# Gated DeltaNet inverse: D product of the first level in 32-column tiles, and a chunk's two token products as one matmul

## The chip, the cores and the metric

The kernel runs on one core of one Trainium2 chip. The metric is the device time of an execution in microseconds (us).

## What is computed

The reference is one inference step of a two-layer hybrid trunk of width 2048: a gated DeltaNet layer, then a Mamba-2 SSD layer, for a prompt of 256 tokens and for 8 sequences of 4 new tokens each. The change lies in the DeltaNet layer's work on the prompt. For each of 16 key heads (two value heads each), in chunks of tokens, it is

```python
a_mat = einsum("bnhid,bnhjd->bnhij", k_beta, k) * decay * strict
t_mat = triangular_solve(eye + a_mat, eye, lower=True, unit_diagonal=True)
u = t_mat @ (v * beta);  w = t_mat @ (k_beta * exp(g))
qk = einsum("bnhid,bnhjd->bnhij", q, k) * decay
```

and then a recurrence over the chunks. The products of keys with keys and of queries with keys, and the inverse of a unit triangular matrix, are what the two edits touch.

## The kernel before

Each engine has its own program, written out by hand, with semaphores between them. The DeltaNet stage is a loop over heads m: 15 turns of a loop and a last head written out behind it. All projections go through the same steps: a half tile of weights (128 x 1024) arrives by DMA, ScalarE takes its upper part (L826), GpSimd (POOL) the rest (L336), and TensorE (PE) does three matmuls of 288 columns for each of 16 slices (L381 to L383, in `project`).

PE's loop counts 48 steps e in a head. In each it does `project` for two slices (six matmuls), and behind it, by the number of the step, a piece of the head's own work in `gdn_mix`. So everything on PE has one order. The pieces that matter here:

- e = 0: token products. `gKN` holds the normalised queries and keys (first index 0 and 1) with 128 rows and the tokens as columns; NC = 2 chunks of CH = 128 tokens. Per chunk there is a transpose of the keys to psA (L446), a product of keys with keys to psC (L447) and one of keys with queries to psC from column 256 on (L448); then a small product for the new tokens (L449), which raises `g_tok`. The vector engine (DVE) multiplies both into its arrays at L1582 and L1586.
- e = 5: transposes of `gDE` to psB (L455), which ScalarE copies (L1017).
- e = 7 to 18: the inverse, in six levels lv, over four matrices u (two chunks, two value heads). At e = 7 + 2 lv PE does the P product to psC (`inv_p`). DVE masks it (`mask_p`, L1609). At e = 8 + 2 lv PE does the D product to psA and then the E product to psE (`inv_q`), and DVE subtracts them (`less_q`, L1621 and L1628). Between these DVE puts independent taps of a convolution (L1600). `do.link` makes DVE's next instruction wait for the end of the one that is linked.
- e = 8 also has, ahead of the D product of the first level, two small transposes of 32 rows (L460).

All three products of the levels 0 to 4 go through one helper, whose matmul is L408:

```python
def blocks(bank, u, lhsT, rhs, lv, n=64):
    for r in range(0, P, n):
        mm = pe.matmul(bank[r:r + n, u * 32:(u + 1) * 32], lhsT[:, r:r + n], rhs[:, in_block(r, lv), :],
                       start=True, stop=True)
```

The output rows r to r + n are a column tile of the array. The P product has n = 32, the D and E products n = 64; each matmul has 32 moving columns. In the profile "128*64" is contraction rows by weight columns of one matmul. A fp32 matmul appears there as two passes, each with its own weight load (PEld); a transpose appears as one.

Of the kernel before, what the change touches and what calls it, by code (L numbers as in the profile page):

```python
# [30 lines left out]
CH = 128  # L31
NC = SEQ // CH
# [62 lines left out]
def bc(ap, axis, n):  # L95
    a = ap.unsqueeze(axis)
    shape = list(a.shape)
    shape[axis] = n
    return a.to_broadcast(shape)


def half(ap, lv, odd):

    v = ap.rearrange("p j (i k s) -> p j i k s", k=2, s=2 << lv)
    return v[:, :, :, odd, :]
# [7 lines left out]
def in_block(r, lv):  # L113

    n = 32 // (2 << lv)
    return slice(r // 64 * n, r // 64 * n + n)
# [25 lines left out]
def build(nc, weights, x_in, p_in, prm_in, cst_in, gpack, spack, gstate, sstate,  # L142
          y_out, gconv_out, sconv_out, gst_p, gst_s, sst_p, sst_s,
          g_rows, s_rows, h_spill, G_DVE, G_ACT, S_DVE, S_ACT):
    with ExitStack() as ctx:
# [3 lines left out]
        def sem(name):  # L149
# [17 lines left out]
        psA, psB, psC, psD, psE, psF = (  # L167
            ctx.enter_context(nc.psum_tensor(f"ps{c}", [P, 512], F32)) for c in "ABCDEF")
# [25 lines left out]
        gKN = ga["KN"].rearrange("p (i t) -> p i t", i=2)  # L194
# [21 lines left out]
        gP = [gPP, gPZ[:, 0], gPZ[:, 1], gPZ[:, 2], gPW, gPW]  # L216

        gDE = ga["DE"].rearrange("p (k u t) -> p k u t", k=2, u=4)
# [73 lines left out]
        def S(name):  # L292
            if name not in sems:
                sems[name] = sem(name)
            return sems[name]
# [74 lines left out]
        def _(pe):  # L370
# [34 lines left out]
# [5 lines that stand above are left out]
                return mm  # L410
# [28 lines left out]
            def gdn_mix(m, e, more):  # L439

                if e == 0:
                    pe.wait_ge(S("g_kn"), m + 1)
                    pe.wait_ge(S("g_y"), m + 1)
                    for c in range(NC):
                        k_c, q_c = (gKN[:, n, c * CH:(c + 1) * CH] for n in (1, 0))
                        pe.transpose(psA[:, c * P:(c + 1) * P], k_c, ident)  # L446
                        pe.matmul(psC[:, c * CH:(c + 1) * CH], k_c, k_c, start=True, stop=True)  # L447
                        pe.matmul(psC[:, 256 + c * CH:256 + (c + 1) * CH], k_c, q_c, start=True, stop=True)  # L448
                    pe.matmul(psE[0:NS, 0:2 * NS], gKN[:, 1, SEQ:T], gKN[:, 0:2, SEQ:T], start=True, stop=True) \  # L449
                        .then_inc(S("g_tok"), 1)  # L450
                if e == 5:
                    pe.wait_ge(S("g_e1"), m + 1)
                    for c in range(NC):
                        for j in range(2):
                            mm = pe.transpose(psB[:, (2 * c + j) * P:(2 * c + j + 1) * P], gDE[:, 1, 2 * c + j, :],  # L455
                                              ident)
                    mm.then_inc(S("g_dt"), 1)
                if e == 8:
                    for j in range(2):
                        mm = pe.transpose(psD[0:NS, 384 + NS * j:384 + NS * (j + 1)], gATS[:, j, :], ident[0:NS, 0:NS])  # L460
# [17 lines left out]
                def inv_q(lv):  # L478


                    pe.wait_ge(S("g_pm"), m * 6 + lv + 1)
                    if lv < 5:
                        for u in range(4):
                            mm = blocks(psA, u, gDE[:, 1, u, :], half(gP[lv], lv, 0)[:, u], lv)
                        mm.then_inc(S("g_qd"), 1)
                    for u in range(4):
                        E = half(gDE[:, 1], lv, 1)[:, u]
                        if lv < 5:
                            mm = blocks(psE, u, gP[lv][:, u, :], E, lv)
                        else:  # L490
                            mm = pe.matmul(psE[0:64, u * 64:(u + 1) * 64], gP[lv][:, u, 0:64], E, start=True, stop=True)
                    mm.then_inc(S("g_qe"), 1)

                for lv in range(6):
                    if e == 7 + 2 * lv:
                        inv_p(lv)
                    if e == 8 + 2 * lv:
                        inv_q(lv)
                if e == 10:
                    for j in range(2):  # L500
                        mm = pe.matmul(psD[0:NS, 256 + NS * j:256 + NS * (j + 1)], gATS[:, j, :], gAS[:, j, :],
                                       start=True, stop=True)
                    mm.then_inc(S("g_sample_pe"), 1)
                if e == 15:
                    for j in range(2):
                        mm = pe.matmul(psD[NS * j:NS * j + NS, 320:320 + NS], gBS[:, j, :], gNS[:, j, :],
                                       start=True, stop=True)
                    mm.then_inc(S("g_sample_pe"), 1)
                if e == 18:
# [5 lines left out]
                    for b in range(DEC_B):  # L515
                        for j in range(2):
                            mm = pe.matmul(psD[64 * j:64 * j + 64, 0:P], gMKQ[:, b, :], gS[:, b, j, :],
                                           start=(b == 0), stop=(b == DEC_B - 1))
                    mm.then_inc(S("g_sample_pe"), 1)
                if e == 17:  # L520
# [3 lines left out]
                    for c in range(NC):  # L524
                        for j in range(2):
                            mm = pe.transpose(psB[:, (2 * c + j) * P:(2 * c + j + 1) * P],
                                              gCR[:, 2 + j, c * CH:(c + 1) * CH], ident)
# [12 lines left out]
                if e == 23:  # L540
                    pe.wait_ge(S("g_es"), m + 1)
                    pe.wait_ge(S("g_rss"), m + 1)
                    for j in range(2):
                        rows = slice(NS * j, NS * j + NS)
                        mm = pe.matmul((psA, psB)[j][:, 0:P], gES[rows], gVBS[rows], start=True, stop=True)
# [10 lines left out]
                if e == 27:  # L556
                    pe.wait_ge(S("g_rhs"), m + 1)
                    new_values(1)
                    for j in range(2):
                        mm = pe.matmul(psD[NS * (2 + j):NS * (3 + j), 256:256 + P], gQKS[:, j, :],  # L560
                                       gVNS[:, j * P:(j + 1) * P], start=True, stop=True)
# [3 lines left out]
                if e == 29:  # L565
# [3 lines left out]
                    for j in range(2):  # L569
                        o = psF[:, (2 + j) * P:(3 + j) * P]  # L570
                        pe.matmul(o, gQD[:, j, :], gS1[:, j, :], start=True, stop=False)
                        mm = pe.matmul(o, gQK[:, 2 + j, :], gVN[:, 2 + j, :], start=False, stop=True)
                    mm.then_inc(S("g_o"), 1)
                if e == 30:
# [4 lines left out]
                    for r in range(2):  # L579
                        for g in range(4):  # L580
                            rows = slice(NS * g, NS * g + NS)
                            mm = pe.matmul((psA, psB, psC, psD)[g][:, r * 256:(r + 1) * 256], gKM[rows, r, :],
                                           gVNDS[rows, :], start=True, stop=True)
                    mm.then_inc(S("g_sp"), 1)
                if e == 41:
                    pe.wait_ge(S("g_on"), m + 1)
                    for j in range(2):
                        for c in range(NC):
# [3 lines left out]
                              start=True, stop=True).then_inc(S("g_ont"), 1)  # L592
# [15 lines left out]
            for n in range(4):  # L608
                for c in range(NC):
                    src = HRG[0:GV, (7, 6, 4, 5)[n], c * CH:(c + 1) * CH]  # L610
                    at = (n * NC + c) * GV
                    mm = pe.transpose(psD[:, at:at + GV], src, ident[0:GV, 0:GV])
            for n in range(5):
                src = HRG[0:GV, (7, 6, 4, 8, 5)[n], SEQ:T]
                for g in range(4):
                    mm = pe.matmul(psD[NS * g:NS * g + NS, 256 + n * GV:256 + (n + 1) * GV], src, ident[0:GV, 0:GV],
                                   start=True, stop=True)
            mm.then_inc(S("g_ccol"), 1)
            with pe.Fori(0, GH - 1) as m:
                for e in range(48):  # L620
                    if e % 8 == 0:
                        bank_wait_act(m, 6, T_GLOOP + e // 8, T_GPRO, TA_G)
                    gdn_ready(m, e)
                    project(m, 6, T_GLOOP + e // 8, e % 8)
                    gdn_mix(m, e, True)

            for e in range(48):
                k = e // 8
                if e % 8 == 0:
                    if k < 4:  # L630
                        bank_wait_act(0, 0, T_GEND + k, T_GPRO, TA_G)
                    else:
                        pe.wait_ge(took_dve, TD_O1 + (k - 3))
                if e < 16 or e >= 20:
                    gdn_ready(GH - 1, e if e < 16 else e - 4)
                project(0, 0, T_GEND + k, e % 8, fresh=X0["oa1"] if k == 2 else None)
                if e < 16:
                    gdn_mix(GH - 1, e, False)
                elif e >= 20:
                    gdn_mix(GH - 1, e - 4, False)  # L640
# [142 lines left out]
            for k in range(2, 7):  # L783
# [4 lines left out]
                if k == 4:  # L788
                    pe.wait_ge(S("s_hrows"), 1)
                    for n in range(3):  # L790
                        for c in range(NC):
                            src = HRG[0:SH, (4, 6, 5)[n], c * CH:(c + 1) * CH]
                            at = (n * NC + c) * SH
                            mm = pe.transpose(psA[:, at:at + SH], src, ident[0:SH, 0:SH])
# [631 lines left out]
        def _(dve):  # L1426
# [136 lines left out]
            def u4(ap):  # L1563
                return ap.rearrange("p (c j) t -> p c j t", c=NC)
# [12 lines left out]
            def gdn_body(m, full):  # L1577

                dve.wait_ge(S("g_tok"), m + 1)
                kk = bc(psC[:, 0:256].rearrange("p (c t) -> p c t", c=NC), 2, 2)  # L1580
                qk = bc(psC[:, 256:512].rearrange("p (c t) -> p c t", c=NC), 2, 2)
                do.link(dve.tensor_tensor(u4(gAT[:, :, :]), u4(gAT[:, :, :]), kk, ALU.mult))  # L1582
                do.link(dve.tensor_tensor(gPW, gAT[:, :, :], bc(cst[:, K_M1, :], 1, 4), ALU.mult))
                dve.tensor_tensor(gDE[:, 1], bc(ident, 1, 4), gPW, ALU.subtract) \
# [194 lines left out]
            with dve.Fori(0, GH - 1) as m:  # L1779
                do.enter(m, G_DVE)  # L1780
                gdn_body(m, True)
                dve.wait_ge(took_act, m * 6 + 12)
            do.leave(GH - 1)
            gdn_body(GH - 1, False)


# [432 lines left out]
```

## Time and profile before

| | |
|---|---|
| median of 3 runs | 2421.05 us (2419.09 to 2421.67) |
| profiled execution | 2421.49 us |
| its span, first to last instruction | 2419.7 us |
| mean granted TensorE clock | 0.989 |
| PE, weight loads | 2327.6 and 2183.3 us busy |
| DVE, ACT, POOL | 1615.2, 1263.9 and 1795.1 us busy |

The page is one profiled execution. Busy shares are over the whole span; the DeltaNet loop is the part from about 83 to 1035 us. In a timeline row several instructions of a kind that follow each other are merged, with their count; the time in the row then goes from the first start to the last end.

### The profile page before, as it was taken

What the parts mean: (1) busy time and instruction counts of PE and PEld (TensorE: products, weight loads), DVE (VectorE), ACT (ScalarE), POOL (GpSimd) and SP (SyncE); (2) the same over time, 40 slices, a digit from 0 to 9 for tenths busy, and PEclk for the clock granted to TensorE, in tenths of its full rate; (3) what the DMA queues carried; (4) which work ended last, traced back from release to release, by engine and by line L of the source; (5) the groups of instructions that cost most, each with busy time, mean ns of one, the idle gap of its engine ahead of it and who ended that gap; (6) DMA issues with size and microseconds to landing.
All of it is one profiled execution on the core that took longest, in us unless ns stands there. A gap on an engine that the chain in (4) does not pass through costs nothing.

```text
span 2419.7 us, 59342 instructions
## 1 busy us (share of the span) xinstructions
PE 2327.6 (96%) x21792; PEld 2183.3 (90%) x21792; DVE 1615.2 (67%) x3171; ACT 1263.9 (52%) x2204; POOL 1795.1 (74%) x2284
## 2 busy tenths in 40 slices
PE   5899999999999999999999979999999999999997
PEld 5799999999999999989999978999999999899997
DVE  7667666666666676661217576988899889703375
ACT  4555555555555555543336456555555555433452
POOL 4566666565555556558889967988898889798896
PEclk9999999999999999999999989999999999999998
DMA  5444444444444444436454446766676657454443
GB/s 197 156 150 156 157 152 154 148 150 144 147 154 150 146 142 148 147 120 220 153 169 148 160 150 205 233 207 192 205 244 212 203 185 240 173 194 156 155 155 117
DMA packets 126775, 410.88 MB, mean 170 GB/s; under 512 B 21344, under 2 KB 37984, under 8 KB 122112
## 3 DMA queue, kind: packets, MB, share of 16 engines
q1 hardware_dynamic: 80784, 294.49, 36.6%
q10 hardware_dynamic: 45936, 115.64, 14.2%
q8 instruction: 37, 0.61, 0.1%
q14 instruction: 18, 0.15, 0.0%
HBM read 363.47 MB, written 46.61 MB: 169 GB/s over the span
## 4 chain that ended last, share of the span: by engine, by line
POOL 37%; PE 32%; issue 23%; DVE 6%; ACT 1%; POOLq 0%; DMA 0%; DVEq 0%; ACTq 0%
POOL wl L336 36%; PE psj L381 9%; PE psj L383 9%; PE psj L382 9%; POOL h L344 1%; DVE h L2003 1%; PE psE L403 1%; PE psE L747 1%; PE psA L721 1%; PE psA L773 1%; DVE arena L1876 0%; DVE arena L1526 0%; DVE arena L2034 0%; DVE xl L1810 0%; DVE xl L1451 0%
## 5 line engine op out<-in xcount | busy, mean ns | idle before, releaser
L336 POOL TENSOR_TENSOR wl<-ring,wh 128x256 fp32r<-128x256 f32 x2232 | 1761.9, 824 | 602.5 <-ACT wh L826 602.2
L381 PE MATMUL psj<-xh,wh 128*128 128x288 f32 x4400 | 1356.9, 308 | 32.6 <-DVE xl L1451 16.5
L382 PE MATMUL psj<-xl,wh 128*128 128x288 f32 x4400 | 1304.1, 296 | 0.0
L383 PE MATMUL psj<-xh,wl 128*128 128x288 f32 x4400 | 1299.3, 295 | 0.0
L381 PEld LDWEIGHTS psj<-xh,wh 128*128 128x128 f32 x4400 | 830.6, 189 | 84.5 <-issue 43.9
L826 ACT ACTIVATE wh<-ring 128x1024 fp32r<-128x1024 f32 x558 | 586.6, 1059 | 600.4 <-PE psj L383 529.4
L382 PEld LDWEIGHTS psj<-xl,wh 128*128 128x128 f32 x4400 | 833.4, 189 | 1.9
L383 PEld LDWEIGHTS psj<-xh,wl 128*128 128x128 f32 x4400 | 834.1, 190 | 0.0
L907 ACT ACTIVATE arena<-psj 128x256 f32<-128x256 f32 x112 | 42.8, 382 | 191.9 <-PE psj L383 186.2
L1802 DVE TENSOR_TENSOR h<-h,psj 128x288 f32 x32 | 14.5, 454 | 155.6 <-PE psj L383 155.6
L1876 DVE SCALAR_TENSOR_TENSOR arena<-arena 128x256 f32<-128x256 f32 x144 | 111.2, 799 | 3.4
L1600 DVE SCALAR_TENSOR_TENSOR arena<-arena 128x256 f32<-128x256 f32 (+1 forms) x192 | 103.5, 559 | 4.1
L1792 DVE COPY Y<-psj 128x288 f32 x22 | 10.1, 458 | 131.5 <-PE psj L383 131.5
L1526 DVE SCALAR_TENSOR_TENSOR arena<-arena 128x256 f32<-128x256 f32 x192 | 80.7, 481 | 1.6
L1497 DVE TENSOR_TENSOR arena<-arena 128x288 f32<-128x288 f32 x45 | 29.4, 653 | 72.2 <-ACT arena L1184 66.5
L1609 DVE TENSOR_TENSOR arena<-psC,cst 64x128 f32<-64x128 f32 (+1 forms) x176 | 53.0, 301 | 21.4 <-PE psC L408 12.0
L2003 DVE TENSOR_TENSOR h<-h,arena 128x512 f32<-128x512 f32 x64 | 63.6, 994 | 0.0
L408 PEld LDWEIGHTS psA<-arena 128*64 128x64 f32 x1280 | 43.8, 137 | 18.6 <-DVE arena L1609 15.0
L408 PE MATMUL psA<-arena 128*64 128x32 f32 x1280 | 52.7, 225 | 4.9 <-DVE arena L1609 4.0
L1621 DVE TENSOR_TENSOR arena<-arena,psA 64x128 f32<-64x128 f32 x160 | 45.7, 285 | 15.0 <-PE psA L408 6.7
L408 PE MATMUL psE<-arena 128*64 128x32 f32 x1280 | 51.0, 223 | 0.0
L408 PEld LDWEIGHTS psE<-arena 128*64 128x64 f32 x1280 | 44.2, 138 | 0.0
(344 smaller groups left out, 2943.5 us busy)
## 6 DMA issues: line engine op xcount, KB each, us to landing
ring<-weights_d SPq DMA_DIRECT2D x558, 512.0 KB, 3.3
h<-gstate_d ACTq DMA_DIRECT2D x16, 1024.0 KB, 7.0
gst_s_d<-h ACTq DMA_DIRECT2D x16, 1024.0 KB, 3.9
h<-sstate_d ACTq DMA_DIRECT2D x32, 512.0 KB, 5.6
sst_s_d<-h ACTq DMA_DIRECT2D x32, 512.0 KB, 5.1
arena<-g_rows_d ACTq DMA_DIRECT2D x16, 864.0 KB, 5.8
arena<-s_rows_d ACTq DMA_DIRECT2D x8, 1152.0 KB, 8.4
h_spill_d<-h ACTq DMA_DIRECT2D x2, 2304.0 KB, 8.2
```

What stands on the lines that cost most here:

```text
L336: ins = pool.tensor_tensor(wl[:, s, n:n + 2], ring[:, s, n:n + 2], wh[:, s, n:n + 2].bitcast(F32), ALU.subtract)
L381: pe.matmul(out, w_h, xh[:, kt, :], start=(kt == 0), stop=False)
L382: pe.matmul(out, w_h, xl[:, kt, :], start=False, stop=False)
L383: mm = pe.matmul(out, w_l, xh[:, kt, :], start=False, stop=(kt == KT - 1))
L408: mm = pe.matmul(bank[r:r + n, u * 32:(u + 1) * 32], lhsT[:, r:r + n], rhs[:, in_block(r, lv), :], start=True, stop=True)
L826: act.activation(wh[:, hc % 4], ring[:, hc % 4], ACT.Copy).then_inc(wh_ready, 1)
L1526: ins = dve.scalar_tensor_tensor(out, src, tap(i, j), out, ALU.mult, ALU.add)
L1600: return dve.scalar_tensor_tensor(out, gU[:, 2 + i, at:at + b - a], gpc_tap[1][:, i, j:j + 1], out, ALU.mult, ALU.add)
L1609: ins = dve.tensor_tensor(half(gP[lv][rows], lv, 0)[:, :, blk, :], packed(psC[rows, 0:(P if lv < 5 else 2 * P)], lv), half(bc(cst[rows, K_ ...
L1621: ins = dve.tensor_tensor(D, D, packed(psA[rows, 0:P], lv), ALU.subtract)
L1876: ins = dve.scalar_tensor_tensor(out, src, w, out, ALU.mult, ALU.add)
L2003: do.link(dve.tensor_tensor(sS[:, b], sS[:, b], bc(sEGb[:, :, b], 2, HD), ALU.mult))
```

## The change

Two edits. The D product of the first level (lv = 0) is made with n = 32, in four column tiles for each matrix, in place of two. And for each chunk one matmul takes the keys as weights and moves queries and keys (256 columns) past them, in place of two matmuls with 128 columns each; its output lies in psC as query part and key part, chunk by chunk, and DVE's two reads of it have the new strides.

```diff
--- before.py
+++ after.py
@@ -442,10 +442,10 @@
                     pe.wait_ge(S("g_kn"), m + 1)
                     pe.wait_ge(S("g_y"), m + 1)
                     for c in range(NC):
-                        k_c, q_c = (gKN[:, n, c * CH:(c + 1) * CH] for n in (1, 0))
+                        k_c = gKN[:, 1, c * CH:(c + 1) * CH]
                         pe.transpose(psA[:, c * P:(c + 1) * P], k_c, ident)
-                        pe.matmul(psC[:, c * CH:(c + 1) * CH], k_c, k_c, start=True, stop=True)
-                        pe.matmul(psC[:, 256 + c * CH:256 + (c + 1) * CH], k_c, q_c, start=True, stop=True)
+                        pe.matmul(psC[:, c * 256:(c + 1) * 256], k_c, gKN[:, 0:2, c * CH:(c + 1) * CH],
+                                  start=True, stop=True)
                     pe.matmul(psE[0:NS, 0:2 * NS], gKN[:, 1, SEQ:T], gKN[:, 0:2, SEQ:T], start=True, stop=True) \
                         .then_inc(S("g_tok"), 1)
                 if e == 5:
@@ -481,7 +481,7 @@
                     pe.wait_ge(S("g_pm"), m * 6 + lv + 1)
                     if lv < 5:
                         for u in range(4):
-                            mm = blocks(psA, u, gDE[:, 1, u, :], half(gP[lv], lv, 0)[:, u], lv)
+                            mm = blocks(psA, u, gDE[:, 1, u, :], half(gP[lv], lv, 0)[:, u], lv, 32 if lv < 1 else 64)
                         mm.then_inc(S("g_qd"), 1)
                     for u in range(4):
                         E = half(gDE[:, 1], lv, 1)[:, u]
@@ -1577,8 +1577,7 @@
             def gdn_body(m, full):
 
                 dve.wait_ge(S("g_tok"), m + 1)
-                kk = bc(psC[:, 0:256].rearrange("p (c t) -> p c t", c=NC), 2, 2)
-                qk = bc(psC[:, 256:512].rearrange("p (c t) -> p c t", c=NC), 2, 2)
+                qk, kk = (bc(psC[:, :].rearrange("p (c n t) -> p c n t", c=NC, n=2)[:, :, n, :], 2, 2) for n in range(2))
                 do.link(dve.tensor_tensor(u4(gAT[:, :, :]), u4(gAT[:, :, :]), kk, ALU.mult))
                 do.link(dve.tensor_tensor(gPW, gAT[:, :, :], bc(cst[:, K_M1, :], 1, 4), ALU.mult))
                 dve.tensor_tensor(gDE[:, 1], bc(ident, 1, 4), gPW, ALU.subtract) \
```

## Rows read from the trace of the kernel before

**Rows 1.** The page: engines, and the chain that ended last by engine

```profile
PE 2327.6 (96%) x21792; PEld 2183.3 (90%) x21792; DVE 1615.2 (67%) x3171; ACT 1263.9 (52%) x2204; POOL 1795.1 (74%) x2284
...
POOL 37%; PE 32%; issue 23%; DVE 6%; ACT 1%; POOLq 0%; DMA 0%; DVEq 0%; ACTq 0%
```

**Rows 2.** Windows by stage: us, busy time and instructions by engine, clock, DMA, GB/s

```profile
83.00:1035.00 952.00, 942.03 (x11286) 862.61 (x11285) 660.41 (x1733) 540.39 (x1045) 581.78 (x768) 1.00 0.45 151
```

**Rows 3.** Waits of 83 to 1035 us: us in total, times, longest

```profile
PEld psA L408 <- DVE arena L1609: 14.0, 44, 0.5
...
DVE arena L1621 <- PE psA L408: 5.7, 19, 0.9
```

**Rows 4.** Timeline, token products, head 7: start, us, engine, line, passes [idle, releaser]

```profile
467.64 0.29 PE L383 MATMUL psj<-xh,wl 128*128 128x288 f32 x1
467.77 0.27 PE L446 MATMUL psA<-cst,arena 128*128 128x128 f32 x1
467.88 0.39 PE L447 MATMUL psC<-arena 128*128 128x128 f32 x2
468.11 0.39 PE L448 MATMUL psC<-arena 128*128 128x128 f32 x2
468.33 0.27 PE L446 MATMUL psA<-cst,arena 128*128 128x128 f32 x1
...
468.66 0.39 PE L448 MATMUL psC<-arena 128*128 128x128 f32 x2
468.98 0.30 PE L449 MATMUL psE<-arena 128*32 128x64 f32 x2
```

**Rows 5.** Timeline of PE, same head: a two-pass product with 256 columns

```profile
511.95 0.59 PE L567 MATMUL psE<-arena 128*128 128x256 f32 x2
512.38 0.38 PE L571 MATMUL psF<-arena 128*128 128x128 f32 x2
512.60 0.39 PE L572 MATMUL psF<-arena 128*128 128x128 f32 x2
```

**Rows 6.** Timeline of the same head, first level of the inverse

```profile
475.41 0.46 PE L408 MATMUL psC<-arena 128*32 128x32 f32 x32
...
475.95 0.60 DVE L1609 TENSOR_TENSOR arena<-psC,cst 64x128 f32<-64x128 f32 x2 [0.66 <-PE psC L408]
...
476.57 1.03 DVE L1600 SCALAR_TENSOR_TENSOR arena<-arena 128x256 f32<-128x256 f32 x1
...
476.79 0.23 PE L460 MATMUL psD<-cst,arena 32*32 32x32 f32 x2
...
476.95 0.66 PE L408 MATMUL psA<-arena 128*64 128x32 f32 x16
...
477.44 0.64 PE L408 MATMUL psE<-arena 128*64 128x32 f32 x16
477.74 0.58 DVE L1621 TENSOR_TENSOR arena<-arena,psA 64x128 f32<-64x128 f32 x2
...
478.35 0.59 DVE L1628 TENSOR_TENSOR arena<-arena,psE 64x128 f32<-64x128 f32 x2
...
478.97 0.65 DVE L1600 SCALAR_TENSOR_TENSOR arena<-arena 128x32 f32<-128x32 f32 x1
...
479.74 0.59 DVE L1609 TENSOR_TENSOR arena<-psC,cst 64x128 f32<-64x128 f32 x2
```

**Rows 7.** Timeline of weight loads for psA, L408: heads 1, 8 and 10

```profile
99.69 0.55 PEld L408 LDWEIGHTS psA<-arena 128*64 128x64 f32 x16
...
110.20 0.55 PEld L408 LDWEIGHTS psA<-arena 128*64 128x64 f32 x16 [0.16 <-DVE arena L1609]
...
539.90 0.55 PEld L408 LDWEIGHTS psA<-arena 128*64 128x64 f32 x16
...
550.90 0.55 PEld L408 LDWEIGHTS psA<-arena 128*64 128x64 f32 x16 [0.48 <-DVE arena L1609]
...
665.79 0.55 PEld L408 LDWEIGHTS psA<-arena 128*64 128x64 f32 x16
```

## The prediction, made before the changed kernel was built or run

> **What bounds the kernel now.** I read the page first: TensorE (the engine PE) is busy for 96% of the span [rows 1]. Both edited places lie in the head loop of the DeltaNet stage, so the second view was the windows by stage. From 83 to 1035 us PE is busy for 942.0 of 952 us at full granted clock, and POOL for 582 [rows 2]. The page's chain gives POOL the largest share [rows 1]; in this stage that is not the bound, because POOL has 370 us of the 952 left over. The loop goes at the pace of PE's own queue.
>
> The third view was the list of waits. Two entries matter in the edited steps. The weight loads of the bank psA at L408 waited for the vector engine's mask at L1609 44 times, 14.0 us in all, and the vector engine waited at L1621 for the same bank 19 times, 5.7 us [rows 3]. So inside the inverse the two engines take turns in being late, and it has to be worked out which of them an edit there speeds up.
>
> **Part 1, token products.** Now a chunk has one transpose (a single pass) and two products of two passes each, five passes of 128 moving columns. The first chunk runs from 467.77 to 468.33 us, thus 0.56/5 = 0.112 us a pass [rows 4]. The change removes the two passes of L448 and makes those of L447 256 columns wide. What a 256-column pass costs is not seen at this line, but at L567: its two passes run from 511.95 to 512.38, thus 0.215 us each, and the pair after it, of 128 columns, takes 0.22 us, or 0.11 each [rows 5]. So a fp32 pass is paid by its moving columns, and what is saved is only what each pass has on top. Per head: 8 x 0.112 = 0.90 us become 4 x 0.215 = 0.86 us, **0.04 us less**. With 0.11 in place of 0.112 it is 0.02. I take 0.04; the bounds are 0 and 0.06. The weight load that disappears was hidden under the pass before it and is costed at nothing. Were it not hidden, the whole pass could be saved (first rival).
>
> Nothing takes these 0.04 us back. The products stand in PE's queue, the products of the first level come 7.5 us later, and there the vector engine waits for PE (0.66 us of idle time at 475.95) [rows 6], so its chain moves forward by the same 0.04 us. L1582 and L1586 read as many elements of psC as before, at another stride: nothing, with bounds of 0.02 us either way, and there is that idle time of 0.66 us to cover it.
>
> **Part 2, D product of the first level.** Now it is 16 passes with 64 columns of weights, which hold PE from 476.95 to 477.44, 0.49 us. The changed one has the shape of the P product, 32 passes with 32 columns of weights. That one stands at 475.41 with 0.46 us for all, of which a single pass is 0.20: the last starts about 0.26 us after the first [rows 6]. Behind it the tile shape changes from 32 to 64 columns for the E product in psE. The nearest row for that change is the one from L460 to L408, 0.16 us with its two passes [rows 6]; the low end is L449, which comes 0.32 us behind the pair before it, where a pair takes 0.22, so 0.10 us [rows 4]. Now no such change stands between the two products; the one between L460 and the D product exists in both kernels. So the phase becomes 0.26 + 0.13 = 0.39 us (0.13 between the two ends), **0.10 us less on PE**.
>
> The Trainium skill has a rule against this edit: in "TensorEngine Tiling (Array Packing)", section Tiling Modes, a change of tiling mode (not of tile alone) drains TensorE. The trace agrees in kind, with the 0.16 us above. If draining meant that the last pass ends (0.20 us) before the next load begins, the phase would be about 0.26 + 0.36 = 0.62 us, and the E product would come 0.13 us later than now; by the next paragraph only the first head would feel it, and the sum would be 0.2 us higher.
>
> **How much of it stays on the path.** The vector engine's chain from the first mask on is: mask 475.95 to 476.55, tap 476.57 to 477.60, D subtraction from 477.74 [rows 6]. The tap has nothing to do with the D product, and the next linked tap (478.97 to 479.62) shows 0.12 us from its end to the start behind it (479.74), where PE had long been done. So the D subtraction can start at 477.72: 0.02 us earlier, with bounds of 0 and 0.14. From there to the mask of the fourth level this engine goes from one instruction to the next, and PE waits for it. The D products of the first and the fourth level stand 11.00 us apart (539.90 and 550.90), in the first head, where the vector engine keeps up, 10.51 us (99.69 and 110.20) [rows 7]. So PE loses 0.49 us a head there; the 0.48 us of idle time in the last row has some 0.16 in it that the change of tile shape takes anyway, as the first head's row shows. So whatever PE gains in the first level is added to that loss: of the 0.10 us about 0.08 is given back at the second to fourth level, and **0.02 us a head** stay. Only the first head keeps all of it. The same slack covers a longer drain: the E product ends at 478.08 and its subtraction starts at 478.35, when the D subtraction has ended.
>
> **Sum.** 16 x (0.04 + 0.02) = 0.96, and 0.08 for the first head: about 1.0 us less. The stages after the loop start that much earlier and are otherwise as before. The profiled execution took 2421.49 us (span 2419.7), which is 0.4 above the median of the runs shown, so the sum holds for the median as well: 2421.05 - 1.0 = 2420.0 us. These three runs lie 2.6 us apart, so the effect is smaller than their scatter.
>
> **Rivals.**
> First, a merged pass is cheaper than I think: if the 0.112 us of a 128-column pass were set by its weight load, a 256-column pass would cost the same and L448's four passes a head would go entirely: 4 x 0.112 x 16 = 7.2 us, with part 2 7.6: 2413.4 us, faster. For it speaks that the projections move 288 columns in 0.13 us [rows 4], which is more than twice as fast by column. Against it speaks L567, fp32 operands as here, at 0.215 us a pass. Chance 4%. The Trainium skill gives this rival its rule: "TensorE: Matmul & The Clock Gate", Back-to-back issue gap and LDWEIGHTS, has N/2.4 + 2.5 ns for N columns and P/1.2 ns for P columns of weights, so 109 ns for 256 columns and 107 for the load, and by these figures the merge would halve the cost. The rows of this trace are about twice that for fp32.
>
> Second, the gain of part 2 stays on the path in every head, because the vector engine's chain isn't what the masks wait for: 16 x (0.04 + 0.10) = 2.2 us, 2418.8 us, the same within the measurement. The 11.00 against 10.51 us speaks against it. 8%.
>
> Third, slower: the passes of the D product with 32-column tiles don't overlap four at a time as those of psC do. At the pitch of the present ones (0.49/16 = 0.031 us) 32 take 0.98 us, the D subtraction begins 0.46 us later and moves the whole chain to the fourth level: 16 x (0.46 - 0.04) = 6.7 us more, 2427.8 us. It decides from a pitch of 0.015 us on, where the last of 32 passes starts later than the last of 16 does now; over 0.2% takes 0.34 us a head, a pitch of 0.026. The same product with the same tiles, strides and column counts has a pitch of 0.008 us in rows 6. Chance 3%.
>
> Fourth, the edit does nothing: the merged product costs as much as the two (0.215 against 2 x 0.11), and the 0.02 us are lost too. 2421.0 us. Chance 23%. My own case has 58%. The remaining 4% are for something that I don't see, half of it of either sign and over 0.2%.
>
> **Numbers.** What a measurement of this kernel can tell from no change is 0.2%, 4.8 us. My case and the second and fourth rival are within it: same 0.58 + 0.08 + 0.23 = 0.89; faster 0.04 + 0.02 = 0.06; slower 0.03 + 0.02 = 0.05. The range has to hold my case, the fourth and most of the second, and the scatter of a median (about 1.3 us each side): 2417.2 to 2422.6.
>
> **What would show it.** Right: L447 twice a chunk with 256 columns, about 0.54 us from one transpose to the next; the D product of the first level as 32 passes in some 0.26 us, then a gap of 0.10 to 0.16 us to psE; D subtraction at most 0.03 us earlier after its tap; the wait for L1609 at the fourth level longer by about 0.08 us; the head, now (665.79 - 539.90)/2 = 62.95 us [rows 7], shorter by 0.06. Wrong: 256-column passes near 0.11 us, D products 11.0 us apart as now while the head is 0.14 us shorter, or a D subtraction later than 0.14 us behind its tap.

## The result and the profile after

Forecast was 2420.0 us (2417.2 to 2422.6), with 0.89 on no change. Measured: **2539.06 us** (2537.05 to 2542.51, 5 runs) against 2419.3 us of the kernel before on the same chip (2418.3 to 2421.67, 5 runs), a ratio of **1.0493, 95% interval 1.0481 to 1.0504**. The profiled execution has a span of 2540.7 us, 121 more than before. The forecast is wrong by 119 us, far outside its range.

From the page of the kernel after: the span, the engines, and the DMA queues (queue, kind, packets, MB, share).

```profile
span 2540.7 us, 59726 instructions
...
PE 2364.7 (93%) x21984; PEld 2204.9 (87%) x21984; DVE 1575.4 (62%) x3171; ACT 1263.2 (50%) x2204; POOL 1777.0 (70%) x2284
...
q8 instruction: 164, 2.69, 0.4%
```

The same queue on the page of the kernel before:

```profile
q8 instruction: 37, 0.61, 0.1%
```

TensorE is busy for 93% in place of 96% [rows 1]. Of the 121 us it is idle for 84 and busy for 37 (2364.7 us against 2327.6). It executes 192 more passes, and each is recorded twice (weight load and matmul), which is the 384 more instructions of the span line. The third line is the one that gives the answer away: 127 more packets that carry instructions.

The waits of TensorE from 83 to 1155 us, the head loop of the kernel after (us in total, times, longest):

```profile
PE psj L382 <- issue: 31.6, 14, 3.5
PE psj L381 <- POOL wl L336: 31.2, 7, 5.0
PE psj L381 <- issue: 27.6, 7, 6.0
```

None of these three is in that stage before. Together they are 90 us; "issue" means that the engine waited for nothing that the profile shows. Fourteen is the number of returns to the start of the loop (15 turns). Half of the returns are put down to POOL, since its semaphore was the last that the profile knows; they last longer, but stand at the same place.

The branch that closes the loop has a row of its own (ns of one: shortest, median, longest; the shortest is the last of the 15, which doesn't return). In this kernel:

```profile
L619 PEldq COMPARE_BRANCH  x15: 83/6317/8143, 149.5 to 1154.4; - x15
```

and in the kernel before:

```profile
L619 PEldq COMPARE_BRANCH  x15: 76/208/234, 149.9 to 1031.2; - x15
```

So a return takes 6.3 us in place of 0.2. TensorE idles for less than that, since matmuls that were issued before the branch are still to be done. One return in its timeline:

```profile
509.48 0.29 PE L383 MATMUL psj<-xh,wl 128*128 128x288 f32 x1
513.38 0.45 PE L381 MATMUL psj<-xh,wh 128*128 128x288 f32 x1 [3.60 <-issue]
513.63 0.44 PE L382 MATMUL psj<-xl,wh 128*128 128x288 f32 x1
513.87 0.44 PE L383 MATMUL psj<-xh,wl 128*128 128x288 f32 x1
514.11 0.44 PE L381 MATMUL psj<-xh,wh 128*128 128x288 f32 x1
517.45 0.40 PE L382 MATMUL psj<-xl,wh 128*128 128x288 f32 x1 [2.90 <-issue]
517.65 0.44 PE L383 MATMUL psj<-xh,wl 128*128 128x288 f32 x1
```

The first row is the last matmul of a head. Then comes nothing for 3.6 us, four matmuls, and nothing again for 2.9 us, in the middle of six matmuls that wait for nothing. And the matmuls between and behind are slow. The windows around it (us, busy time of PE, PEld, DVE, ACT and POOL with counts, granted clock, DMA share, GB/s):

```profile
502.00:509.50 7.50, 7.50 (x57) 7.26 (x56) 5.66 (x10) 5.98 (x13) 7.12 (x10) 1.00 0.80 282
509.50:513.30 3.80, 0.28 (x3) 0.04 (x1) 0.31 (x1) 1.80 (x4) 3.80 (x6) 1.00 0.92 306
513.30:521.00 7.70, 4.72 (x18) 3.50 (x19) 0.41 (x1) 0.38 (x1) 3.23 (x5) 0.56 0.61 200
521.00:530.00 9.00, 9.00 (x138) 8.49 (x137) 5.86 (x17) 3.29 (x6) 5.68 (x8) 1.00 0.17 62
```

After the first gap the granted clock is 0.56 of full speed, nearly the lower of its two levels (1.2 of 2.4 GHz), until about 521 us. The token products fall into this stretch: a 256-column pass at L447 takes 631 ns at the median in this kernel, and 379 at full clock.

The page Runtime: NRT & Kernel Launch of the Trainium skill (section Instruction fetch mechanics) says that TensorE's instruction memory holds 128 KiB, 2048 instructions, and is filled in blocks of 16 KiB, 256 instructions, and that a taken branch whose target is not in the blocks at hand has to wait for a fetch. The packets agree with the block: 2.69 MB over 164 is 16.4 KB. So the theory that the experiments test is about the place of the code. I counted TensorE's program (a weight load and a matmul for each pass, every wait and register instruction one):

- The whole program of before is 9661 instructions, 37.7 blocks, and its page has 37 packets, about one for each block: the loop was not fetched again. The changed one has 9709 instructions and 164 = 38 + 14 x 9 packets.
- The loop was 1548 instructions and is now 1572, which is also the number of TensorE's records from one branch to the next (32 more for the D product, 8 fewer for the token products).
- The second stall marks a block's edge: it lies between the weight load and the matmul of the second L382, eleven instructions behind the loop's start. So the loop starts at place 245 of a block. The loop of before then reaches one instruction into its eighth block, and the changed one 25.

### The profile page after: what moved, and what is told of

Read it like the earlier page. It is cut to its first block, busy times and chain, and to the rows that moved or that the text cites. A ratio compares the mean times of both kernels' runs of the same rounds, so it can differ in the third digit from the quotient of the medians.

```text
span 2540.7 us, 59726 instructions
## 1 busy us (share of the span) xinstructions
PE 2364.7 (93%) x21984; PEld 2204.9 (87%) x21984; DVE 1575.4 (62%) x3171; ACT 1263.2 (50%) x2204; POOL 1777.0 (70%) x2284
## 3 DMA queue, kind: packets, MB, share of 16 engines
q8 instruction: 164, 2.69, 0.4%
## 4 chain that ended last, share of the span: by engine, by line
POOL 35%; PE 34%; issue 26%; DVE 3%; ACT 1%; POOLq 0%; DMA 0%; ACTq 0%; DVEq 0%
POOL wl L336 33%; PE psj L381 10%; PE psj L383 10%; PE psj L382 10%; POOL h L344 1%; PE psA L773 1%; PE psE L403 1%; PE psE L747 1%; PE psA L721 1%; DVE arena L1526 0%; DVE xl L1809 0%; DVE xl L1451 0%; PE psB L727 0%; PE psC L727 0%; ACT xh L845 0%
## 5 line engine op out<-in xcount | busy, mean ns | idle before, releaser
L336 POOL TENSOR_TENSOR wl<-ring,wh 128x256 fp32r<-128x256 f32 x2232 | 1740.7, 815 | 741.6 <-ACT wh L826 740.9
L382 PE MATMUL psj<-xl,wh 128*128 128x288 f32 x4400 | 1313.3, 298 | 31.6 <-issue 31.6
L383 PE MATMUL psj<-xh,wl 128*128 128x288 f32 x4400 | 1308.6, 297 | 0.0
L383 PEld LDWEIGHTS psj<-xh,wl 128*128 128x128 f32 x4400 | 842.0, 191 | 33.1 <-issue 33.1
L382 PEld LDWEIGHTS psj<-xl,wh 128*128 128x128 f32 x4400 | 841.7, 191 | 1.9
L1581 DVE TENSOR_TENSOR arena<-arena,psC 128x512 f32<-128x512 f32 x16 | 11.0, 688 | 153.2 <-PE psE L449 152.9
L1599 DVE SCALAR_TENSOR_TENSOR arena<-arena 128x256 f32<-128x256 f32 (+1 forms) x192 | 89.6, 488 | 4.1
L408 PE MATMUL psE<-arena 128*64 128x32 f32 x1280 | 51.4, 223 | 0.0
L408 PEld LDWEIGHTS psA<-arena 128*64 128x64 f32 (+1 forms) x1536 | 40.6, 128 | 12.3 <-DVE arena L1608 6.3
```

The source lines that it names most:

```text
L336: ins = pool.tensor_tensor(wl[:, s, n:n + 2], ring[:, s, n:n + 2], wh[:, s, n:n + 2].bitcast(F32), ALU.subtract)
L382: pe.matmul(out, w_h, xl[:, kt, :], start=False, stop=False)
L383: mm = pe.matmul(out, w_l, xh[:, kt, :], start=False, stop=(kt == KT - 1))
L1599: return dve.scalar_tensor_tensor(out, gU[:, 2 + i, at:at + b - a], gpc_tap[1][:, i, j:j + 1], out, ALU.mult, ALU.add)
```

## The experiments

The waits that are put ahead of the loop in some kernels stand at the very start of TensorE's program and are satisfied long before; two of them in the source make one instruction (the span line of e3, with twelve, has 6 instructions more than that of before). They change nothing but the place of all that follows. Four kernels first.

**e1_tokens_alone.** The changed kernel without

```diff
-                            mm = blocks(psA, u, gDE[:, 1, u, :], half(gP[lv], lv, 0)[:, u], lv, 32 if lv < 1 else 64)
+                            mm = blocks(psA, u, gDE[:, 1, u, :], half(gP[lv], lv, 0)[:, u], lv)
```

> Three theories. A, place of the code: TensorE's program for the head loop is fetched again in every head once it no longer lies in seven blocks of 256 instructions; in the kernel before it ends, by my count, just at the end of its seventh block. B, size of the code: the loop is fetched again once it has more than some number of instructions between 1548 (before) and 1572 (changed), wherever it lies. C, no fetching: the 32-column tiles of the D product, or the 256-column product, cost 8 us a head themselves. This kernel has the token products alone, 1540 instructions in the loop. A and B: as fast as before, by my prediction's term 0.6 us less, 2418.7, within 0.1% of before, and no more instruction packets than the 37 of before. C, if it is the token products: over 2500 us; if it is the D product, as A.

Measured: 2420.55 us, ratio 1.0001 (0.9992 to 1.0010), 37 instruction packets. The token products don't cost anything, and by this measurement bring nothing either.

**e2_d_tiles_alone.** The kernel before with the other edit:

```diff
-                            mm = blocks(psA, u, gDE[:, 1, u, :], half(gP[lv], lv, 0)[:, u], lv)
+                            mm = blocks(psA, u, gDE[:, 1, u, :], half(gP[lv], lv, 0)[:, u], lv, 32 if lv < 1 else 64)
```

> The D product of the first level in 32-column tiles alone, 1580 instructions in the loop, 32 more than before. A and B: slow, about 2539 us and some 160 instruction packets. C: slow if the D product is what costs, with instruction packets near 37 and the time lost around e = 8; fast if it is the token products.

Measured: 2540.82 us, 1.0511 (1.0495 to 1.0527), 164 packets. This alone fits all but the theory that the token products cost.

**e3_before_six_waits_ahead.** The kernel before, none of its products touched:

```diff
+            for _ in range(12):
+                pe.wait_ge(c_in, 16)
             pe.wait_ge(c_in, 16)
             pe.wait_ge(S("prm_in"), 16)
```

> The kernel before, without either edit, with six waits on a semaphore long satisfied put at the start of TensorE's program, ahead of the loop. The loop has the same 1548 instructions, six places later. A: it now reaches six instructions into an eighth block, so slow, about 2535 to 2545 us, with some 160 instruction packets. B and C: as before, 2419.3 us, since neither the loop's size nor any product has changed.

Measured: 2545.57 us, **1.0519 (1.0503 to 1.0535)**. From its page, and from the list of TensorE's waits over its whole span (two of the nine put down to POOL lie outside the loop):

```profile
q8 instruction: 163, 2.67, 0.4%
```

```profile
PE psj L382 <- issue: 43.8, 14, 4.3
PE psj L381 <- POOL wl L336: 36.2, 9, 5.0
PE psj L381 <- issue: 25.5, 7, 3.9
```

Six satisfied waits, executed once, cost 126 us. That ends theory C, and B too: the loop has its 1548 instructions. The second stall has moved as it must if it marks a block's edge: six places earlier, to the first L382's matmul, five instructions behind the loop's start.

**e4_changed_sixteen_waits_ahead.** Both edits, and the same lines with `range(32)`.

> The changed kernel, both edits, with sixteen such waits ahead of the loop, which moves the loop's start just past a block's edge: 1572 instructions from place 4 of a block, so within seven blocks. A: fast, 2418.3 us (2416 to 2421), with the 1.0 us of my prediction's sum as the only difference to before, and about 37 instruction packets. B and C: slow, about 2539 us.

Measured: 2419.76 us, **1.0002 (0.9993 to 1.0011)**, and on its page

```profile
q8 instruction: 38, 0.62, 0.1%
```

So the changed kernel's 120 us are gone when its loop starts sixteen places later, at place 5 of a block. Theory A stands, by a kernel without the change that is slow and a kernel with it that is not.

**Where the edge is.** e5 is e3 with `range(2)`, one instruction; e6 and e7 are e4 with `range(22)` and `range(24)`, eleven and twelve instructions.

> The kernel before with a single wait ahead of the loop. From the second stall in the changed kernel's head (twelve instructions behind the loop's start) and my count of 1548 in the loop, the loop of before should end exactly on the edge of its seventh block. A with that place: one instruction over the edge is enough, slow, 2535 to 2550 us, about 163 instruction packets. A with the count a few places off: fast, 2420, and 37 packets.

> The changed kernel with eleven waits ahead: by the same count the loop starts at the last place of a block and touches eight blocks. Slow, 2535 to 2550 us, about 163 packets. If the edge lies elsewhere: fast.

> The changed kernel with twelve waits ahead: by the same count the loop starts at the first place of a block and touches seven. Fast, 2417 to 2421 us, 37 or 38 packets. Together with the eleven waits this places the edge to one instruction.

Measured, one run each: 2429.47, 2419.18 and 2419.22 us, with 46, 38 and 38 packets. e7 came as expected. e6 did not: when I wrote these expectations I took the edge one place too late, from the weight loads alone, where the stall seems to stand at L383. The matmul row of L382 above shows it one instruction earlier, and then e6 starts at the first place of a block. e5 is neither: its TensorE waits show one slow return of 14,

```profile
PE psj L381 <- issue: 3.9, 1, 3.9
...
PE psj L382 <- issue: 2.3, 1, 2.3
```

and 46 = 37 + 9 packets say the same. Three further kernels asked what lies between one instruction and six: e9 is e3 with `range(6)`, three instructions; e10 is e5 again; e11 is e4 with `range(16)`, eight instructions.

> The kernel before with three waits ahead of the loop. With one wait 1 of 14 returns to the loop's start was slow, with six all 14. A, in the form that the last instructions of the loop race with a fetch that evicts the loop's first block, so that the edge is a few instructions wide: between the two or like six, 2430 to 2546 us, with 46 to 163 instruction packets, and each slow head about 8.8 us longer than 62.95 while the others stay at 62.95. B and C: 2420.

> The same kernel as e5, timed again. If the edge is a race, its runs scatter more than those of before (5 us): some multiple of 8 to 9 us over 2420 in each run, so from 2419 to 2460, with a median of about 2430. If it is a fixed place that was passed once for another reason, all runs within 3 us.

> The changed kernel with eight waits ahead. Eleven were fast, none slow. By the loop before, which ends not more than a few places past an edge, the changed loop now starts 1 to 3 places ahead of a block's edge and touches eight blocks: slow, over 2530 us and about 163 packets. Fast if the loop of before ends four or more places past the edge.

Measured: e9 2528.64 us (2516.99 to 2537.16, ratio 1.0431, 1.0399 to 1.0462), 145 packets, 12 slow returns. e10: ten runs from **2418.81 to 2464.46**, median 2428.99; the ratio, which leaves out the run of 2464.46, is 1.0025 (1.0005 to 1.0044). Its profiled execution, which took 2451.21 us, has 3 slow returns and 64 packets. e11: 2551.16 us in its one run, 164 packets. All by the place:

| kernel | instructions in the loop | start, place in its block | past the edge of the 7th block | slow returns of 14 | packets |
|---|---|---|---|---|---|
| e1 | 1540 | 245 | -7 | 0 | 37 |
| before | 1548 | 245 | 1 | 0 | 37 |
| e5, e10 | 1548 | 246 | 2 | 1 and 3 | 46 and 64 |
| e9 | 1548 | 248 | 4 | 12 | 145 |
| e3 | 1548 | 251 | 7 | 14 | 163 |
| changed | 1572 | 245 | 25 | 14 | 164 |
| e2 | 1580 | 245 | 33 | 14 | 164 |
| e11 | 1572 | 253 | 33 | 14 | 164 |
| e6, e7, e4 | 1572 | 0, 1, 5 | -220, -219, -215 | 0 | 38 |

Each slow return has nine packets, and each slow head is 8 to 12 us longer than the 62.95 of the others, from 70.9 to 75.2 us in e9 to e11. The edge is a few instructions wide: with two past it the return is slow now and then, with seven always. e10 came as forecast, in its scatter too. That is what a race between the branch and a fetch that has been begun looks like; what the fetcher does inside is not shown by these runs.

**Can the tiles bring more where the code fits?** e8, with sixteen instructions ahead:

```diff
-                            mm = blocks(psA, u, gDE[:, 1, u, :], half(gP[lv], lv, 0)[:, u], lv, 32 if lv < 1 else 64)
+                            mm = blocks(psA, u, gDE[:, 1, u, :], half(gP[lv], lv, 0)[:, u], lv, 32)
...
-                            mm = blocks(psE, u, gP[lv][:, u, :], E, lv)
+                            mm = blocks(psE, u, gP[lv][:, u, :], E, lv, 32 if lv > 2 else 64)
```

> The changed kernel with sixteen waits ahead, the D product in 32-column tiles in all levels 0 to 4 and the E product in levels 3 and 4 too: 1764 instructions, which from place 4 of a block still lie in seven blocks. A, and the gain of tiles given back only where the vector engine's chain holds PE up (levels 0 to 2): D and E together take 0.44 us less on PE (16 passes in 0.49 us become 32 in 0.27, twice) at levels 3 and 4, of which the vector engine takes back some 0.2 at level 4: 0.6 to 0.7 us a head, 2409 us (2407 to 2413). If that engine takes back all but what lies behind its last mask: 2415. B (size of the loop): slow, over 2500 us.

Measured: 2417.74 us, 0.9991 (0.9982 to 1.0000), 39 packets. The lowest median of all, though the interval reaches 1.0, and 9 us above the forecast. Its timeline of TensorE, levels 4 and 5:

```profile
553.34 0.46 PE L408 MATMUL psA<-arena 128*32 128x32 f32 x32
553.61 0.49 PE L408 MATMUL psE<-arena 128*32 128x32 f32 x32
555.61 0.68 PE L477 MATMUL psC<-arena 128*64 128x64 f32 x8 [0.53 <-DVE arena L1622]
```

The two products behave as assumed (0.27 us apart, where they were 0.49 [rows 6]). But now TensorE waits 0.53 us ahead of the product of the last level, for the vector engine's D subtraction of level 4. That engine's chain reaches further than I had it: through the whole inverse, and most of the gain is given back there: a head takes 62.85 us, 0.10 less than before, in place of 0.6 to 0.7 less.

**A loop that never fits.** e12 is e8 with `32` in place of `32 if lv > 2 else 64`: 1860 instructions, from place 5 on 73 past the edge.

> The changed kernel with sixteen waits ahead and 32-column tiles in the D and E products of all five levels: 1860 instructions, 7.27 blocks, so no place makes it lie in seven. A: slow, about 2535 us, some 163 to 180 packets, the head at 71 to 73 us as in the changed kernel although TensorE has up to 1 us a head less to do. If only the count of 24 instructions or the place mattered: fast.

Measured: 2446.92 us in one run, and 166 packets (10301 instructions are 40 blocks, and 14 x 9 more). The packets came as expected, the time didn't: it fetches as often as the changed kernel and loses 26 us against the kernel before, not 120. Its windows around one return, with the same columns as before:

```profile
530.00:539.00 9.00, 9.00 (x68) 8.77 (x67) 7.12 (x16) 6.99 (x14) 7.65 (x11) 1.00 0.59 198
539.00:541.00 2.00, 0.70 (x6) 0.47 (x5) 0.62 (x2) 1.39 (x4) 2.00 (x3) 1.00 1.06 422
541.00:550.00 9.00, 9.00 (x93) 8.23 (x94) 5.73 (x11) 2.95 (x7) 9.00 (x12) 1.00 0.71 231
```

and its timeline of weight loads at the same place:

```profile
540.87 0.19 PEld L381 LDWEIGHTS psj<-xh,wh 128*128 128x128 f32 x1 [1.53 <-issue]
```

At the return there is one stall of 1.5 us in place of two of 3.6 and 2.9, and the clock stays at full speed in this stretch. But that is not all of its loss. The waits of TensorE in its loop (83 to 1100 us) have an entry that those of e8 have not, and the timeline shows what it is:

```profile
PE psE L408 <- issue: 23.1, 25, 1.6
```

```profile
361.26 0.27 PE L408 MATMUL psE<-arena 128*32 128x32 f32 x7
362.62 0.41 PE L408 MATMUL psE<-arena 128*32 128x32 f32 x25 [1.09 <-issue]
```

That is a gap within 32 passes that wait for nothing. Counted in TensorE's records, this gap stands 507 instructions behind the loop's start, and another of 1.37 us in the same head stands 763 behind it. The edges lie at 251, 507 and 763. So e12 pays at later edges too, 23 us in all.

Two things differ by place: this loop has 73 instructions to do behind the edge before it branches, and the next edge comes 251 instructions after the return, not 11. Its branch takes 3.5 us at the median, where it took 6.1 in e3 with 7 behind the edge and 5.8 in e2 with 33, so that from 7 to 33 the first of the two makes little difference. Whether the rest comes from the 73 or from the distance of the next edge was not tried alone.

## Why the prediction was wrong

**The step that failed** is in the part "How much of it stays on the path" and in the sum: "The stages after the loop start that much earlier and are otherwise as before", with nothing in the sum for the number of TensorE's instructions. The D product's 16 passes became 32, which I costed as time on the array alone (0.10 us less), and not as 32 more instructions in a loop body. Of all the rivals none had this mechanism; it sat in the 2% "for something that I don't see". The third rival had the sign, at 2427.8 us, but by passes that don't overlap, and they do.

What the runs put in its place: 14 slow returns at about 8.8 us. In the changed kernel the two small transposes at L460 start first at 99.23 and last at 1166.43 us, before at 99.53 and 1043.31. That is 123.4 us more over 15 heads, of which the last, without a return, is no longer than before (62.34 against 62.94); 123.4/14 = 8.8 us. The stalls are 90 us of it, 6.5 us a return. The other 33 us are TensorE being longer at its passes: it is busy for 975.2 us from 83 to 1155 us, where it was 942.0 in the stage before [rows 2]. The stretch at the lower clock behind each return is where passes take longer.

It could have been read. The page before had the queue of instructions with 37 packets, which is the whole program once, so the loop was being held; and the loop's length, counted, was six blocks and a twentieth. Whether it lay one place or 25 past an edge could not be read from that profile, since without a fetch nothing marks the edge. But a rival "the loop no longer fits where it lies" was due, though no row of before had its price.

**The terms that were right**, seen in e4, where nothing is fetched. Timeline of TensorE, token products and first level:

```profile
467.30 0.27 PE L448 MATMUL psA<-cst,arena 128*128 128x128 f32 x1
467.41 0.60 PE L449 MATMUL psC<-arena 128*128 128x256 f32 x2
467.85 0.27 PE L448 MATMUL psA<-cst,arena 128*128 128x128 f32 x1
```

```profile
476.46 0.46 PE L408 MATMUL psA<-arena 128*32 128x32 f32 x32
476.85 0.66 PE L408 MATMUL psE<-arena 128*64 128x32 f32 x16
```

(The lines put in move TensorE's lines by two; against the kernel before, the vector engine's are moved by one.) From transpose to transpose 0.55 us, forecast 0.54, before 0.56 [rows 4]: a fp32 pass is paid by its moving columns, and the first rival, which had the 256-column pass for the price of one of 128, falls. The D product takes 0.39 us to the start of the E product, forecast 0.39, before 0.49 [rows 6]; the change of tile shape costs its 0.13 us and no more. And the vector engine:

```profile
476.07 1.06 DVE L1601 SCALAR_TENSOR_TENSOR arena<-arena 128x256 f32<-128x256 f32 x1
477.26 0.59 DVE L1622 TENSOR_TENSOR arena<-arena,psA 64x128 f32<-64x128 f32 x2
```

0.13 us from the tap's end to the D subtraction, 0.14 before, so hardly any of the D product's 0.10 us reaches the chain, as forecast. The second rival, that it stays on the path, falls too: the wait for the mask has grown instead, by 0.1 us a head, from 14.0 us in the stage [rows 3] to

```profile
PEld psA L408 <- DVE arena L1610: 15.6, 44, 0.5
```

I had it grow at the fourth level. It grew at the second and is the same at the fourth. The weight loads of psA in head 10, second and fourth level of before, then the first, second and fourth of e4:

```profile
669.22 0.55 PEld L408 LDWEIGHTS psA<-arena 128*64 128x64 f32 x16 [0.17 <-DVE arena L1609]
...
676.77 0.55 PEld L408 LDWEIGHTS psA<-arena 128*64 128x64 f32 x16 [0.49 <-DVE arena L1609]
```

```profile
665.32 0.35 PEld L408 LDWEIGHTS psA<-arena 128*32 128x32 f32 x32
668.79 0.55 PEld L408 LDWEIGHTS psA<-arena 128*64 128x64 f32 x16 [0.30 <-DVE arena L1610]
...
676.35 0.55 PEld L408 LDWEIGHTS psA<-arena 128*64 128x64 f32 x16 [0.49 <-DVE arena L1610]
```

**A second step that failed, too small for the time to show.** I had 0.06 us a head and 1.0 us in all. The head of e4 is (1042.87 - 99.20)/15 = 62.911 us by the same transposes, that of before (1043.31 - 99.53)/15 = 62.919. The 0.01 us between them are mostly the first head, 62.38 us against 62.46, the 0.08 that I had for it. In the others nothing stays, so "Nothing takes these 0.04 us back" is wrong. In the mean of 13 heads the token products bring the start of the small product behind them from 1.204 to 1.179 us after the first transpose, 0.025 less and not 0.04, in e1 and e4 alike. But from that transpose to the P product of the last level it is 25.822 us in before, 25.817 in e1 and 25.823 in e4: by then it is gone. What takes it back is not shown. The ratio's interval, 0.17% wide, can't tell 1.0 us from nothing. So of the four cases of my prediction, the edits alone are nearest to the fourth, no effect.

## What to carry to other kernels

In a loop, an instruction has a second price besides its time on the engine: the body must stay in the instruction memory, and what decided here was how many blocks it touches, its start included: seven, and an eighth by one instruction at most. Before adding instructions to a large body, count it, and compare the packets of the instruction queue with the blocks of the program: about equal means that nothing is fetched again, and a rise by a fixed number for each turn means that the loop has fallen out. The row of the loop's branch shows it too: 0.2 us when nothing was fetched, 3.5 to 6.3 at the median when it was. Where it has by a few instructions, try moving its start with a few idle instructions ahead of the loop before giving up the change; sixteen of them were worth 119 us here.

## What the runs showed that I had not expected

- Six satisfied waits ahead of a loop cost 126 us (e3), and one made the same kernel scatter by 46 us from run to run (e10), where before scatters by 3 to 6. A kernel whose runs scatter like that may stand on such an edge.
- A loop of 1764 instructions stays in place if it touches seven blocks (e8), and one of 1548 doesn't if it reaches seven instructions into an eighth (e3). Seven blocks and one fetched ahead would make eight, the 2048 instructions of the Trainium skill's page named above; what is held at a time no run shows. Its sentence that this memory is only two lines of 16 KiB, 32 KiB in all, doesn't hold for TensorE here: fourteen returns over 1548 instructions fetched nothing, and the branch took 0.2 us each time.
- The same nine fetches a head cost 8.8 us in the changed kernel and about 2 us in e12, whose loop ends and starts at other places of a block and which pays a part of it at later edges. The lower clock behind the stalls is a part of the price which the stalls themselves don't show.
